# A hybrid layer on 8 cores: the second block of x between the scale's quarters, two token-sum matmuls, and another order of work

## The reference

```
h   = x * (1 + scale1) + shift1         scale, shift, gate from silu(cond) @ w_ada + b_ada
P   = h @ w_in                          columns: q k v g (retention), z xBC dt (SSD)
ret = two-directional retention, 4 heads of 128, chunked scan, RMS norm per head, * silu(g)
ssd = silu(conv5(xBC)); two-directional chunked scan, 8 heads; * silu(z); RMS norm
x   = LN1(ALPHA * x + gate1 * (concat(ret, ssd) @ w_out))
x   = LN2(ALPHA * x + gate2 * SwiGLU(x * (1 + scale2) + shift2))
```

## Time and profile before

| | us |
|---|---|
| runs shown | 743.0, 746.5, 797.92 (median 746.5) |
| the profiled execution | 746.21 |
| its span, slowest core (core 7) | 745.1 |
| spans of the other cores | 737.5 to 743.7 |
| TensorE busy | 693.7 (93%) |
| VectorE, ScalarE, POOL busy | 370.9, 331.2, 265.9 |

### The profile page before, as it was taken

One profiled execution on the slowest core, in us unless ns is written; L12 is line 12 of the kernel. 1 busy time (PEld: TensorE's weight loads), 2 busy tenths in 40 slices (PEclk: granted clock), 3 DMA queues, 4 the chain that ended last, 5 costly groups with the idle time before them and its releaser, 6 DMA issues.

```text
span 745.1 us, 13289 instructions; the slowest of 8 cores (737.5 to 745.1 us)
## 1 busy us (share of the span) xinstructions
PE 693.7 (93%) x4492; PEld 369.4 (50%) x4492; DVE 370.9 (50%) x780; ACT 331.2 (44%) x632; POOL 265.9 (36%) x238
## 2 busy tenths in 40 slices
PE   1659999999999998988999999999999999999995
PEld 1336555755566554545655444444444444444443
DVE  2234545364588989569795221121121110486666
ACT  1234558787878455878887221111111110132222
POOL 9000012256655879976879930200000000000000
PEclk9689999899999999999999999999999999999998
DMA  7999922118683075995016954682443333121102
GB/s 163 154 242 170 129 35 46 38 43 128 100 129 58 1 121 150 263 176 143 1 29 86 182 73 57 78 113 37 56 58 57 57 57 86 56 86 79 63 35 79
DMA packets 64449, 69.22 MB, mean 93 GB/s; under 512 B 6240, under 2 KB 54016, under 8 KB 64384
## 3 DMA queue, kind: packets, MB, share of 16 engines
q0 software_dynamic: 50512, 44.65, 40.1%
q1 hardware_dynamic: 13872, 23.72, 10.0%
HBM read 98.32 MB, written 8.40 MB: 143 GB/s over the span
## 4 chain that ended last, share of the span: by engine, by line
PE 79%; DMA 7%; DVE 6%; issue 4%; ACT 3%; POOL 1%; DVEq 0%; ACTq 0%; another core or an unknown queue 0%; POOLq 0%; SPq 0%
PE psum L440 77%; DMA arena<-w_in 5%; DVE arena L474 5%; PE psum L507 3%; ACT arena L454 2%; POOL arena L501 1%; DMA oret<-arena 1%; ACT L454 1%; DMA arena<-sret 1%; DVE arena L491 0%; POOL arena L479 0%; DVE arena L486 0%; DVE psum L474 0%; POOL arena L474 0%; DVE arena L481 0%
## 5 line engine op out<-in xcount | busy, mean ns | idle before, releaser
L440 PE MATMUL psum<-arena 128*128 128x512 bf16 (+7 forms) x4286 | 668.5, 314 | 23.4 <-ACT arena L454 8.3
L440 PEld LDWEIGHTS psum<-arena 128*128 128x128 bf16 (+1 forms) x4286 | 344.0, 100 | 341.4 <-issue 48.3
L454 ACT ACTIVATE arena<-psum 128x512 bf16<-128x512 f32 (+2 forms) x228 | 129.3, 589 | 241.5 <-PE psum L440 207.8
L474 POOL TENSOR_TENSOR arena<-arena 128x512 bf16<-128x512 bf16 (+3 forms) x154 | 200.0, 1325 | 71.9 <-PE psum L440 25.7
L454 ACT ACTIVATE arena<-arena 128x512 bf16<-128x512 f32 (+8 forms) x261 | 135.7, 540 | 137.3 <-DVE arena L486 63.2
L474 DVE TENSOR_TENSOR arena<-arena,psum 128x512 bf16<-128x512 bf16 (+3 forms) x115 | 83.9, 736 | 207.4 <-PE psum L440 193.5
L474 DVE TENSOR_TENSOR arena<-psum,arena 128x512 f32<-128x512 f32 (+4 forms) x118 | 72.7, 624 | 37.9 <-PE psum L440 34.1
L454 ACT ACT_TABLE_LOAD x34 | 43.6, 1283 | 17.2 <-PE psum L440 6.5
L507 PE MATMUL psum<-arena 128*128 128x128 f32 (+2 forms) x206 | 31.9, 297 | 20.3 <-DMA arena<-x 15.8
L474 DVE TENSOR_TENSOR psum<-psum,arena 128x512 f32<-128x512 f32 (+1 forms) x57 | 37.7, 685 | 25.7 <-PE psum L440 23.5
L454 ACT ACTIVATE arena<-psum,arena 128x512 bf16<-128x512 f32 (+1 forms) x48 | 33.1, 708 | 14.2 <-PE psum L440 11.4
(11 more groups left out here) (19 smaller groups left out, 75.2 us busy)
## 6 DMA issues: line engine op xcount, KB each, us to landing
arena<-w_ada POOLq DMA_DIRECT2D x10, 1024.0 KB, 13.1
arena<-x POOLq DMA_DIRECT2D x6, 1024.0 KB, 43.1
arena<-w_in POOLq DMA_DIRECT2D x6, 1024.0 KB, 14.1
arena<-x SPq DMA_DIRECT2D x12, 512.0 KB, 7.4
arena<-w_gate POOLq DMA_DIRECT2D x11, 512.0 KB, 6.9
arena<-w_up POOLq DMA_DIRECT2D x11, 512.0 KB, 7.7
y<-arena SPq DMA_DIRECT2D x11, 512.0 KB, 2.6
arena<-w_down POOLq DMA_DIRECT2D x5, 1024.0 KB, 8.2
```

The lines of the kernel that those rows point to most:

```text
L440: return P.op(PE, lambda e: e.matmul(out, lhsT=lhsT, rhs=rhs, start=start, stop=stop), [lhsT, rhs], [out], c)
L454: return P.op(ACT, lambda e: e.activation(out=out, in_=in_, func=func, **kw), [in_] + [v_ for v_ in (bias, scale) if isap(v_)], [out] + ([ ...
L474: return P.op(veng(eng), lambda e: e.tensor_tensor(out=out, in0=in0, in1=in1, op=op), [in0, in1], [out], vcost(eng, out, [in0, in1]))
```

## The change

Four things change.

1. The second block of x is loaded between the second and the third quarter. In the loop over quarters, ahead of the third, it is transposed whole, four slices of its h are made with the scale that is there, and twelve matmuls of 512 columns begin sums for three of the four tiles in banks 4 to 6. The last two quarters then go on with both blocks. The fourth tile follows after the loop.
2. The running sums of the decays take two float32 matmuls of 192 columns in place of 24 of 16.
3. In the last tile, q_ and v_ run on POOL.
4. The ordering has new estimates: a cost and a time of occupancy per operation, a latency per pair of engines, a model of the transfers by row size, a rule on TensorE's clock. It runs in a class `Sim`; and the ranks get small random numbers from a table of 26 entries (seed, first and last operation, amplitude).

```diff
+        for seed, lo, hi, amp in VARIED:
+            x = (seed * 2654435761 + 12345) & 0xffffffff
+            for i in range(lo, hi):
+                x = (x * 1664525 + 1013904223) & 0xffffffff
+                pr[i] += amp * ((x >> 8) / 16777216.0)
+        return Sim(ops).run(lambda o: -pr[o.idx])
...
+VARIED = (
+    (524051, 2409, 3409, 0.3),
...
+            elif e == PE and a[0][2].stream < 0.03 and self.recent * math.exp(-(t - self.recent_t) / 2.0) < 0.6:
+                for ent in sorted(a)[:200]:
+                    if ent[2].stream > 0.05 and ent[0] < a[0][0] + 60.0:
+                        pick = ent
...
-    for half in range(2):
-        seq_prio()
-        x_load(1, half)
+        if q == 1:
+            for half in range(2):
+                seq_prio()
+                x_load(1, half)
...
     for q in range(4):
+        if q == 2:
+            x_transposed(1, xTf[:, :, 512:1024])
+            for kt in range(4):
+                h_scaled(kt, 512, 512)
+            for kt in range(4):
+                for j in range(3):
+                    mm(PS(4 + j), wBC[:, kt, j * 128:(j + 1) * 128], hT[:, kt, 512:1024], kt == 0, False)
+            bset[0] = [7]
         mod_slot(wsc[q], 8 + q * 2, 2)
...
             for j in range(4):
                 mm(PS(j), wBC[:, kt, j * 128:(j + 1) * 128], hT[:, kt, 0:512], kt == 0, kt == 7)
+            if q >= 2:
+                h_scaled(kt, 512, 512)
+                for j in range(3):
+                    mm(PS(4 + j), wBC[:, kt, j * 128:(j + 1) * 128], hT[:, kt, 512:1024], False, kt == 7)
...
-    for half in range(2):
-        x_transposed_half(1, half, xTf[:, :, 512:1024])
-        for kt in range(8):
-            h_scaled(kt, 512 + half * 256, 256)
-    for j in range(4):
-        for half in range(2):
-            for kt in range(8):
-                mm(PS(j, 256, half * 256), wBC[:, kt, j * 128:(j + 1) * 128], hT[:, kt, 512 + half * 256:768 + half * 256], kt == 0, kt == 7)
-        xbc_evac(j, 4 + j, 1)
+    bset[0] = [0, 1, 2, 3]
+    for j in range(3):
+        xbc_evac(4 + j, 4 + j, 1)
+    xbc_proj(wBC, 3, 7, 1)
...
-    for b in range(NTT):
-        mm(PS(7, 16, b * 16), utri_f[:], LA[:, b, :], True, True)
-        mm(PS(7, 16, 192 + b * 16), ones_f[:], LA[:, b, :], True, True)
+    LAf = LA.rearrange("p b d -> p (b d)")
+    mm(PS(7, 192), utri_f[:], LAf, True, True)
+    mm(PS(7, 192, 192), ones_f[:], LAf, True, True)
...
-        ts(q_[:, 0:1], s2[:, 0:1], s2[:, o_:o_ + 1], ALU.add, s2=1.0 / 1024.0, op1=ALU.mult)
-        ts(v_[:, 0:1], m_[:, 0:1], m_[:, 0:1], ALU.mult, s2=q_[:, 0:1], op1=ALU.subtract)
+        veng_ = POOL if parts else DVE
+        ts(q_[:, 0:1], s2[:, 0:1], s2[:, o_:o_ + 1], ALU.add, s2=1.0 / 1024.0, op1=ALU.mult, eng=veng_)
+        ts(v_[:, 0:1], m_[:, 0:1], m_[:, 0:1], ALU.mult, s2=q_[:, 0:1], op1=ALU.subtract, eng=veng_)
```

More of the change, by code:

```diff
@@ L34 @@
     __slots__ = ("idx", "eng", "fn", "is_dma", "dsem", "dval", "deps", "inc", "cval", "cost", "fin", "npend", "succ", "start",
-                 "aps", "table", "prio", "nbytes", "out")
+                 "aps", "table", "prio", "nbytes", "out", "occ", "slow", "rowb", "stream")
     def __init__(self, idx, eng, fn, is_dma):
@@ L128, in _record, with op @@
         op.deps = sorted(deps, key=lambda o: o.idx)
-    def op(self, eng, fn, reads, writes, cost, table=None):
+    def op(self, eng, fn, reads, writes, cost, table=None, slow=False):
         o = Op(len(self.ops), eng, fn, False)
-        o.cost, o.table, o.prio = cost, table, self.prio
+        o.occ = {PE: cost, ACT: max(cost - 0.115, 0.09), DVE: max(cost - 0.088, 0.07), POOL: max(cost - 0.05, 0.05), SP: cost}[eng]
+        o.cost = cost + 0.165 if eng == PE else cost
+        o.table, o.prio, o.slow = table, self.prio, slow
         self.ops.append(o)
@@ L166, in schedule @@
                 d.succ.append(o)
[L168 to L175, removed]
         bl = [0.0] * len(ops)
         for o in reversed(ops):
-            m = 0.0
+            m = o.cost
             for s_ in o.succ:
-                v = bl[s_.idx] + lat(o, s_)
+                v = bl[s_.idx] + edge(o, s_)
@@ L182, in schedule @@
                 if v > m:
                     m = v
-            bl[o.idx] = o.cost + m
+            bl[o.idx] = m
         pr = [bl[o.idx] + o.prio for o in ops]
[L186 to L258, removed]
@@ L265, in emit @@
         self.order = order
+        self.est_total = max(o.fin for o in self.ops)
         esem = {e: stack.enter_context(nc.semaphore("c_" + e)) for e in ENGS}
@@ L347, with dma_time, edge @@
 TABWAIT = 6.0
+CLKWIN = 3.4133
+def dma_time(nbytes, rowb):
+    return max(nbytes / rowb * (0.022 + rowb / 27100.0) / 15.5, nbytes / 292e3)
+def edge(d, o):
+    if d.is_dma:
+        return d.cost
+    if d.eng == o.eng:
+        if o.eng == PE and not o.is_dma:
+            return d.occ
+        return d.cost if o.eng != PE else d.occ
+    if o.is_dma:
+        return d.cost + (0.6 if o.eng == POOL else 0.13)
+    if o.eng == PE:
+        return d.cost + 0.15
+    if o.eng == POOL:
+        return d.cost + (0.2 if d.eng == ACT else 0.14)
+    return d.cost + 0.1
@@ L460, in vcost, with vslow @@
         if eng == POOL:
-            return 0.07 + n_ * 0.00225
-        if n_ <= 16:
-            return 0.12
+            return 0.08 + n_ * 0.00222
         if any(inps(a) for a in ins):
             return 0.15 + n_ * 0.00105
-        if all(a.dtype == BF16 for a in list(ins) + [out]):
-            return 0.1 + n_ * 0.00085
-        return 0.1 + n_ * (0.0015 if len(ins) > 1 else 0.00105)
+        if n_ <= 16:
+            return 0.2
+        if len(ins) > 1:
+            return 0.15 + n_ * (0.0009 if out.dtype == BF16 else 0.00116)
+        return 0.15 + n_ * 0.00088
+    def vslow(eng, ins):
+        return eng == DVE and len(ins) > 1 and not any(inps(a) for a in ins)
     def veng(eng):
@@ L487, in stt @@
                     [in0, in1] + [v_ for v_ in (scalar,) if isap(v_)], [out] + ([] if accum_out is None else [accum_out]),
-                    vcost(DVE, out, [in0, in1]))
+                    vcost(DVE, out, [in0, in1]), slow=vslow(DVE, [in0, in1]))
     def cp(out, in_, eng=DVE):
```

191 lines of the change are left out of this document (179 added, 12 removed).

## The result

The changed kernel takes 734.7 us (median of 4 runs, 734.3 to 735.8) against 745.2 us before: 0.986 of it, 95% interval 0.983 to 0.988. (Any kernel here is now and then slowed by a lower clock of one die, as in the run of 797.92 us; such runs are left out of ratios.) Run again later beside the last three experiments it gave 0.9883 [0.9864, 0.9903], 8.7 us of 743.3. It is faster by 1.2 to 1.4%. The predicted time, 735 us, was met; the steps that led there were only partly right, and part of the hit is luck.

A forecast was written before the change was run, and what follows sets the result against it. Bounds: a transfer-bound start, a slow place near 140 us, 12.5 us of scattered TensorE waits, a short tail. Sum -1.5 - 5.8 - 3.5 - 0.3 = -11.1 us on 745.1, 734.0; plus 1.1 beyond the span, 735 us; range 726 to 746.

The forecast's parts named there:

- Two token-sum matmuls, -5.8: Running sums of the decays: two wide matmuls for 24 small ones save 5.8 us, the middle of 3.7 and 7.9.
- the upper bound, 7.9: Token sums: 5.9 us less TensorE time plus 2.0 us from a 2.4 GHz clock there, in all 7.9 us.
- the lower bound: Token sums: if TensorE's work comes sooner, ScalarE can shorten the stretch behind by at most 3.7 us.
- ScalarE over 90% busy behind it: Expected sign: ScalarE, 89% busy in the 35 us behind the token sums, would pass 90% there.
- The order of work, -3.5: All engines reordered: TensorE's idle 1.2 and 2.3 us at 182-220 and 300-345 us can be reached, 3.5 us gained.
- The bounds of 12.5 us to either side: Order of work: it can take all 12.5 us of TensorE's scattered waits from 62 to 735 us, or add as many.
- Its case without the order, 738.6 us: Whole kernel: the order does nothing of what it is there for, the rest is kept; 738.6 us, inside the forecast.
- The start, -1.5: Start: second block's work fits into waits for x and w_in, removing 1.5 us of late matmuls after the second w_in.
- near 62 us: Expected sign at the start: the second w_in still releases TensorE near 62 us, with only its 512-column matmuls behind.
- The tail, -0.3: Last tile: two small operations on POOL save 0.3 us, between 1.1 us gained and 0.8 us lost.
- ScalarE takes the place of the small matmuls: Rival: 3.7 us gained at the token sums, nothing from order or tail; 739 to 746 us, say 742; chance 0.17.
- Slower by collisions: Rival: VectorE's 128x1024 adds collide with POOL, 17 us more; 756 us; decides from 1.7 us per add; chance 0.05.

The follow-up runs named there:

- experiment 7: Kernel before, its order kept on every engine, two 192-column token-sum matmuls where the last of the 24 small ones stood: 737.6 us, 0.9933 of before.
- 9: The changed kernel run again unaltered, as the measure for three runs beside it: 734.7 us, 0.9883 of the kernel before.
- 10: Changed kernel with the old start ordered by the new planner, the changed kernel's order from the first wxs matmul on: 734.3 us, 0.9884 of before.
- experiment 12: Changed kernel with the old start and 24 small token-sum matmuls, its order kept from wxs on; only the tail edit left: 742.7 us, 0.9995 of before.
- 8: Changed kernel, its order kept on every engine, with 24 matmuls of 16 columns in place of the two of 192: 741.5 us, 0.9981 of before.
- experiment 1: Kernel before with the two token-sum matmuls alone, reordered by the old planner: 749.5 us, 1.0092 of before.
- experiment 5: As experiment 1, but POOL issues two weight loads behind the seven adds that followed them: 748.2 us, 1.0082 of before.

## Why the prediction was right, and where its steps were not

**The total.** Predicted -11.1 us; measured -10.6 at first (745.2 to 734.7 us) and -8.7 when run again. Experiments 7 and 9 split the latter: the sums in the old order -5.0, the new order around them another -3.7 (0.9933 to 0.9883; 1.6 to 5.8), the start nothing on the slowest core (10), and the tail nothing by the traces. That 735 us was met is in part luck. The 746.2 us that the terms were taken from is one execution, whose slowest core had its second w_in at 62.27 us; beside the experiments the kernel before took 742.7 to 743.6 us (three medians), and from there the same sum would have given 732. Of the 11.4 us between the two profiled spans, 4.0 lie in the landing of that w_in (62.27 and 58.29 us), which the forecast had left where it was.

**Two token-sum matmuls, -5.8: right in size, too narrow in reasoning.** Measured -5.0 in the old order and -7.3 to -9.3 in the new one; 12 against 10, on one chip, gives -8.3. In the new order the upper bound, 7.9 with the clock's gain, was the better value: 0.8 us for the four records and a clock of 1.00 came as foreseen. In the old order ScalarE did become the next to be late, as the lower bound feared, and took 3.2 us of the gain (waits of 4.9 us before, 8.1 in experiment 7). What failed is the size of that bound, "ScalarE can shorten that stretch by its 3.7 us at most". It counted ScalarE's idle time only behind the sums. Its larger idle time lay beside them: 6.5 us of 11 in experiment 12, 0.1 in 10. "ScalarE over 90% busy behind it" was therefore wrong (27.67 of 35 us), it is full ahead of it.

**The order of work, -3.5: the step that failed, as a term of its own.** It was added as if it stood alone; alone it is worth 0.4 us (-0.4 to 1.1), with the sums 3.7. In experiment 12 TensorE's waits from 62 us on did fall, from 12.5 to 9.2 us, nearly the 3.5 that the term counted, and the time stayed: TensorE was busy for 698.2 us in place of 693.7, of which 1.1 lie in the small matmuls and the rest is not located. With the two wide matmuls the waits are 15.4 us in the old order (7) and 11.7 in the new (9), less by about what the order then gains; these are single traces. Nor was it a matter of small waits alone: with the old planner the same edits cost 3.5 us, and the longest wait there, 7.7 us, stood behind one load of states. The bounds of 12.5 us to either side would have held that. The prediction took the old order as given, though the planner makes another after every edit. Its case without the order, 738.6 us, looks like the 737.6 of experiment 7, but that is 5.0 us off its own kernel before, not 7.6.

**The start, -1.5: right on the mean core, wrong for the metric.** TensorE waits for the second w_in with its work done, as forecast. But the wait ends when that transfer lands, and the slowest core is one where it lands late. The row of 62.27 us was such a core's; 58.29 us is core 6's, 53.44 core 3's. Forecasting w_in "near 62 us" took one core's landing for the kernel's. And the sum had the 17 matmuls behind that wait at 0.225 us each, as before, where the wait was 0.24 us. Behind 2.3 us of idle time they took 5.51 us on the slowest core of the changed kernel and 5.37 on that of experiment 9: 1.5 to 1.7 us more by the clock, as much as the term. That this is why the slowest core gains nothing fits both traces, and no experiment tried it alone.

**The tail, -0.3: nothing.** Neither the 1.1 us of gain came nor the 0.8 of loss: VectorE's pair was not held up, and POOL's two operations cost as much as the waits they avoid (1.60 to 1.61 us to the logarithm in the traces of 8, 9, 10 and 12 as well). The Trainium skill (SBUF — State Buffer, section "SBUF: two separate sides") says that POOL and a VectorE operation with two SBUF inputs keep each other out for a whole instruction. The trace agrees on the 128x1024 adds, which took 0.68 us or, begun while POOL was at an addition, 1.10 to 1.74. In the tail the pair is no longer than in the earlier trace rows (1.42 us); whether POOL's 0.54 and 0.62 us hold a wait can't be told, as no run shows such an operation on POOL with VectorE idle.

**The rivals.** *ScalarE takes the place of the small matmuls* shows in part in experiment 7 (3.2 us of 6.9), and in experiment 1 at a higher price than its 742 us (749.5); the longest wait there was not for ScalarE's tables, it stood behind a transfer. *Slower by collisions* did not happen: the adds took 956 ns on average, far from the 1.7 us from which it decides, though five of the twelve did collide.

## What to carry to other kernels

In a kernel whose order a planner remakes after every edit, an edit's worth is measured only with the order held: replace the instruction in the finished order, then let the planner run, and read the two results apart (here -5.0 and +6.8 us for the same two lines). Beside the engines such an order has a hidden resource, the transfer queues: look for small transfers that are long in flight beside weight loads issued early, and move the loads before calling them the cause (experiment 5). A gain that ends in a wait for a transfer can be worth nothing on the core where that transfer is late, and that core sets the time; look, too, at the clock of what follows the wait. And take the time from which terms are subtracted from several runs, not from the one that was profiled.

## What the runs showed of the hardware

A load of 256 KB took 14.5 us with weight loads of another queue in flight (experiment 1), 6.6 and 8.2 us in experiment 5, 3.7 and 3.9 us before. A POOL operation on 128x1 took 0.54 to 0.62 us, as long as one on 128x128 (0.59); VectorE's took 0.21 to 0.27. The cores of one execution differ by 6 us, with the landing of the start's transfers: from there on each took 674 to 677 us. Five 128x512 adds of POOL stood 3.4 us behind the issue of a transfer whose buffer was not free. A 128x1024 add of VectorE took 0.68 us, or 1.10 to 1.74 when it began during an addition of POOL. After waits of 2.25 to 3.23 us four of eight cores ran 17 matmuls of 512 columns in 5.35 to 5.52 us, partly at the 1.2 GHz level; the other four, after 0.82 to 2.93 us, in 3.83.
